# Turned probabilities in a paged decode attention: one group of 4 or 5 transposes, or one now and the rest a step later

## The chip, the cores and the metric

The kernel runs on one core of one Trainium2 chip. The metric is the device time of one launch in microseconds; the median of the runs is compared. A core has five engines that run their own instruction queues and meet by semaphores: TensorE (PE, its weight loads are shown apart as PEld), VectorE (DVE), ScalarE (ACT), GpSimd (POOL) and SyncE (SP). SP and POOL issue the transfers (DMA) here.

## What is computed

One inference step of a decoder layer for a prompt of 1024 tokens and for 8 sampled sequences of 4 new tokens each, with 8192 past positions in pages of 128. The part that the change touches is the attention of the 32 sampled tokens over their pages, in two branches: A, a softmax over the 256 keys that an indexer selected (here a bias masks the others), and B, a differential attention with two softmaxes per head.

```python
def sample_mixers(...):
    o_a = dsa_attend(qa, qi, wi, qpos, kidx_all, gather_a, topk)      # branch A
    past_b = pool_b_kv[page_table].reshape((B, P) + pool_b_kv.shape[2:])
    ...
    o_b = diff_attend(qb, segments, lam, subln_g, lam_init)           # branch B
    return o_a, o_b
def diff_attend(qb, segments, lam, subln_g, lam_init):
    ...
    p = jax.nn.softmax(jnp.concatenate(scores, axis=-1), axis=-1)
    a = p[:, :, 0] - lam * p[:, :, 1]
    ... outs.append(jnp.einsum('bhqs,bshe->bqhe', a[..., start:start + L], v))
```

Everything is float32. After the attention, a dense tail (two branch projections, the output projection, a SwiGLU block and a per-layer input) runs over all 1056 tokens.

## The kernel before

Six phases run one after the other: `project`, `prompt_select`, `prompt_attend`, `sample_select`, `sample_attend`, `tail`, with a barrier between them. The change is in `sample_attend`, which in the trace lies at about 1520 to 3280 us.

`sample_attend` walks the 8 sequences (batches `b`) in 64 chunks of 8 pages, 8 chunks a batch (`PER` = 8). For a chunk the work is: load the keys of both branches (SP, `load_keys`), transpose them on DVE (`keys`, two parts, line 1723, and `keys_a`, line 1731), multiply with the queries on PE (`scores`, lines 1563 and 1573). Four chunks fill the score banks; then ACT and DVE move them out (`evacuate`). At a batch's end the maximum is found (`top`, `top_rows`, `spread`), and ACT takes the exponentials (`exps`, line 1687). The exponentials lie with the queries on the partitions, and the product with the values wants them turned: `turn` is four 128x128 transposes on PE into the one bank `stat` (line 1603; line 1599 for the new tokens), which ACT then copies to `prob_t` (`prob_out`, line 1701; line 1698 for the new tokens). A batch has 4 such turns for its first half and 5 for its second, plus `sum` on PE (line 1610), which also writes `stat`. Every user of `stat` waits on `stat_read` for the reader of the user before it: `pe.wait_ge(stat_read, use[slot])`.

The product with the values is `values(v, part)` on PE (lines 1626 and 1630), for pages 0 to 3 (part 0) and 4 to 7 (part 1) of chunk v, ten steps (`LAG`) after the chunk's keys. The values of a chunk lie in `ring_v` and `ring_va`, which hold exactly one chunk of 8 pages. POOL loads page n into its place as soon as page n-8 has been used: `pool.wait_ge(v_used, n - RING + 1)`, in order, two transfers a page (lines 1489 and 1490, 256 KB and 64 KB). PE waits before each part for its four pages.

What sets the order on every engine is a list written by hand, `order`: for each of 74 steps the slots `scores`, `keys`, `values`, `turn` and so on. Step s holds the scores of chunk s-1, the keys of chunk s and the values of chunk s-10. Into this list a planner lays the units of the dense tail for two thirds of the tokens (`rest`: lines 1223, 1195, 1201): each slot of a step adds the same part of the step's share to a budget, and a unit is laid in when the budget covers its cost. PE, ACT, DVE and SP all walk the same list. POOL's own list of page loads doesn't follow it.

Names in the rows: `tw_w`, `tw_z`, `tw_x`, `tw_h` and `sa_t` belong to the tail units ("filler" below), `sa_s` to scores, `sa_o` to values, `sa_stat` to the shared bank. A float32 matmul of the source shows as two in the trace, so a filler of 8 in the order is x16 there.

## Time and profile before

| | us |
|---|---|
| median of 3 runs | 3784.25 |
| lowest, highest | 3779.7, 3790.87 |
| the profiled execution, its own time | 3782.91 |
| its span | 3781.3 |
| PE busy in the span | 2949.5 (78%) |
| DVE busy | 1528.3 (40%) |
| POOL busy | 589.5 (16%) |
| ACT busy | 568.1 (15%) |

The span is the profiled part of the execution; 1.6 us of its own time lie around it. Busy shares are means over phases with different limits, so the stretch of `sample_attend` is read by itself. The chain that ended last covers 14% of the span: it goes back through the phase `tail`, whose PE work is 12%, to the barrier before it.

### The profile page before, as it was taken

The numbers are of one execution on the slowest core, as the hardware profiler recorded it, in microseconds if no ns is written. First come the engines' busy times: TensorE is split into PE (matmuls) and PEld (weight loads), VectorE is DVE, ScalarE is ACT, GpSimd is POOL, SyncE is SP. The second block draws the span as 40 slices with busy tenths as digits, with TensorE's granted clock in tenths as the row PEclk, the third lists the DMA queues.
The fourth block names the chain that finished last, engine by engine and source line by source line (L and its number), as shares of the span: only waits on it lengthen the run. The fifth ranks groups of instructions, "written<-read, shape, count | busy, mean of one in ns | idle before, by whom it ended". The sixth has DMA issues, their size and how long they took to land. (4 is left out here: it accounts for less than half of the span.)

```text
span 3781.3 us, 66414 instructions
## 1 busy us (share of the span) xinstructions
PE 2949.5 (78%) x25067; PEld 1904.8 (50%) x25067; DVE 1528.3 (40%) x2849; ACT 568.1 (15%) x1201; POOL 589.5 (16%) x1089
## 2 busy tenths in 40 slices
PE   8999899369956000849888888885989888779998
PEld 4444366246756000525555655553656555446665
DVE  2222399657635883553333234344433201131102
ACT  1111200046634000010101011101101100010001
POOL 0000000000011000003343342333333442000000
PEclk9999699779968555979999989997999999889999
DMA  5232322310033004758989898997899864523333
GB/s 189 93 95 69 102 68 74 97 72 1 1 118 106 0 0 108 232 185 273 292 282 284 263 318 269 307 281 241 269 307 285 266 205 148 149 86 111 111 98 96
DMA packets 631343, 619.29 MB, mean 164 GB/s; under 512 B 64785, under 2 KB 503985, under 8 KB 630930
## 3 DMA queue, kind: packets, MB, share of 16 engines
q1 hardware_dynamic: 569106, 430.81, 37.8%
q0 software_dynamic: 61952, 184.62, 14.5%
q8 instruction: 187, 3.06, 0.4%
q14 instruction: 98, 0.80, 0.1%
HBM read 568.27 MB, written 46.98 MB: 163 GB/s over the span
## 5 line engine op out<-in xcount | busy, mean ns | idle before, releaser
L1223 PE MATMUL sa_t<-tw_z,tw_w 128*128 128x352 f32 x1664 | 559.3, 493 | 24.5 <-DVE tw_z L1301 11.1
L1723 DVE STREAM_TRANSPOSE sa_key_b<-sa_ring_k 128x2048 f32<-128x2048 f32 x128 | 295.2, 2308 | 482.7 <-PE sa_s L1563 244.6
L1489 POOL DMA_DIRECT2D sa_ring_v<-cache_b_kv x512 | 275.6, 538 | 1093.4 <-PE sa_o L1630 724.9
L1223 PEld LDWEIGHTS sa_t<-tw_z,tw_w 128*128 128x128 f32 x1664 | 330.8, 204 | 223.9 <-issue 82.6
L1223 PE MATMUL sa_t<-tw_x,tw_w 128*128 128x352 f32 x960 | 307.2, 479 | 53.8 <-DMA sa_new_sel<-new_bias 35.9
L213 PE MATMUL pr_acc<-pr_w,pr_u_t 128*128 128x512 f32 (+1 forms) x864 | 327.1, 540 | 0.0
L1490 POOL DMA_DIRECT2D sa_ring_va<-cache_a_kv x512 | 275.2, 538 | 53.7 <-issue 26.8
L1223 PEld LDWEIGHTS sa_t<-tw_x,tw_w 128*128 128x128 f32 x960 | 187.0, 198 | 163.2 <-issue 62.8
L1223 PE MATMUL ta_bank<-tp_z,tp_w 128*128 128x352 f32 x832 | 248.8, 462 | 5.6 <-DVE tp_z L1301 4.3
L213 PEld LDWEIGHTS pr_acc<-pr_w,pr_u_t 128*128 128x128 f32 x864 | 152.6, 191 | 168.2 <-issue 168.2
L439 PE MATMUL sel_g<-sel_u,sel_gw 128*128 128x352 f32 x768 | 229.6, 462 | 0.0
L1626 PE MATMUL sa_o<-sa_ring_v,sa_prob_t 128*8 128x128 f32 x4096 | 150.4, 292 | 88.4 <-DMA sa_ring_va<-cache_a_kv 86.5
L1563 PE MATMUL sa_s<-sa_key_b,sa_q_pad 32*32 32x256 f32 x8192 | 185.5, 400 | 31.0 <-DVE sa_key_b L1723 24.0
L1223 PEld LDWEIGHTS ta_bank<-tp_z,tp_w 128*128 128x128 f32 x832 | 159.1, 191 | 95.7 <-issue 8.4
L979 PE MATMUL ss_sums<-ss_count,ss_halves 128*128 128x16 f32 x66 | 20.0, 384 | 223.9 <-DVE ss_count L1052 215.5
L439 PEld LDWEIGHTS sel_g<-sel_u,sel_gw 128*128 128x128 f32 x768 | 147.0, 192 | 83.6 <-issue 3.3
L1626 PEld LDWEIGHTS sa_o<-sa_ring_v,sa_prob_t 128*8 128x8 f32 x4096 | 107.0, 94 | 141.2 <-DMA sa_ring_v<-cache_b_kv 94.5
L511 DVE TENSOR_SCALAR_CACHE_REDUCE sel_hit<-sel_score,sel_edge 128x384 f32<-128x384 f32 (+2 forms) x192 | 168.9, 942 | 3.1
L1563 PEld LDWEIGHTS sa_s<-sa_key_b,sa_q_pad 32*32 32x32 f32 x8192 | 120.1, 105 | 86.9 <-issue 31.4
L1223 PE MATMUL ta_bank<-tp_x,tp_w 128*128 128x352 f32 x480 | 143.8, 462 | 21.1 <-DMA tp_w<-w_br_a 21.1
L979 PEld LDWEIGHTS ss_sums<-ss_count,ss_halves 128*128 128x128 f32 x66 | 16.5, 309 | 227.5 <-DVE ss_count L1052 219.0
L1223 PEld LDWEIGHTS ta_bank<-tp_x,tp_w 128*128 128x128 f32 x480 | 91.9, 192 | 72.5 <-issue 22.3
(322 smaller groups left out, 3308.9 us busy)
## 6 DMA issues: line engine op xcount, KB each, us to landing
sa_ring_k<-cache_b_kv SPq DMA_DIRECT2D x512, 256.0 KB, 5.9
sa_ring_v<-cache_b_kv POOLq DMA_DIRECT2D x512, 256.0 KB, 6.1
tw_w<-w_gate_up SPq DMA_DIRECT2D x88, 512.0 KB, 8.6
sa_ring_ka<-cache_a_kv SPq DMA_DIRECT2D x512, 64.0 KB, 5.7
sa_ring_va<-cache_a_kv POOLq DMA_DIRECT2D x512, 64.0 KB, 5.9
tp_w<-w_gate_up SPq DMA_DIRECT2D x44, 512.0 KB, 3.7
tw_w<-w_down SPq DMA_DIRECT2D x32, 512.0 KB, 6.2
pr_w<-w_in SPq DMA_DIRECT2D x5, 2048.0 KB, 13.5
```

Of the source, the lines that this page charges most:

```text
L213: ins = pe.matmul(acc[c][:, 0:hi - lo], u_t[:, k, :], w[:, k, lo:hi], start=(k == 0), stop=(k == KC - 1))
L439: ins = pe.matmul(g_bank[n % 4][:, 0:PIECE], gw[j % GATE_W][:, k, :], u[:, k, c * PIECE:(c + 1) * PIECE], start=(k == 0), stop=(k == KC - 1))
L511: nc.vector.tensor_scalar(hits(i), of(i, 0, w), edge[:, n:n + 1].bitcast(F32), None, ALU.is_ge, ALU.add, accum_out=count[:, n:n + 1])
L979: pe.matmul(sums[:], halves[:], count[:], start=True, stop=True).then_inc(summed, 1)
L1223: ins = pe.matmul(bank[:, 0:PIECE], self.w[:, at % self.SLOTS, k - lo, :], moving[:, k, :], start=(k == 0), stop=(k == kc - 1))
L1489: pool.dma_start(ring_v[:, n % RING, :], rows_of(cache_b, page, 1)).then_inc(v_in[n // 4 % 2], 16)
L1490: pool.dma_start(ring_va[:, n % RING, :], rows_of(cache_a, page, 1)).then_inc(va_in[n // 4 % 2], 16)
L1563: ins = pe.matmul(s_bank[32 * h:32 * h + 32, k, 0:CH * 32], q_pad[rows, d, h, 24 - 8 * j:56 - 8 * j], key_b[rows, :, 4 * h + d, :], start= ...
L1626: pe.matmul(o_bank[32 * h:32 * h + 8, 0:P], prob_t[:, g, 0, at:at + 8], ring_v[:, g, h * P:(h + 1) * P], start=False, stop=False, tile_pos ...
L1723: nc.vector.transpose(key_b[:, at:at + 4].rearrange("p g n s -> p (g n s)"), ring_k[:, at:at + 4, :].rearrange("p g e -> p (g e)")).then_i ...
```

## The change

In a step whose number leaves 1 or 5 when divided by 8, all 4 or 5 turns of a half batch stood at the end of the step, the `sum` behind the four of the first half. Now only the first turn stands there. The others move to the next step (2 or 6): one directly after the scores, one between the two key parts, the rest and the `sum` after `keys_a`. In these next steps the two `values` parts, which stood between the key slots, come last, one directly behind the other. `finish` and `combine` stay ahead of the first turn. The numbers in `use` follow the list. As the slots of a step share its filler, the filler moves too.

```diff
+            half, turns = {1: (0, 4), 5: (1, 5)}.get(s % PER, {2: (0, 4), 6: (1, 5)}.get(s % PER, (0, 0))) if s > PER and b < NB else (0, 0)
+            begins = s % PER in (1, 5)
+            probs = [("turn", b, half, i) for i in range(turns)]
+            after = [] if begins else probs[1:]
             step = [("scores", s - 1)] if 0 < s <= CHUNKS else []
             step += [("new", b), ("set_q", b + 1)] if ends else []
+            step += after[0:1]
             step += [("keys", s, 0)] if s < CHUNKS else []
+            step += after[1:2]
...
-            step += [("values", s - LAG, 0)] if s >= LAG else []
+            step += [("values", s - LAG, 0)] if s >= LAG and not after else []
             step += [("keys", s, 1)] if s < CHUNKS else []
...
             step += [("keys_a", s)] if s < CHUNKS else []
+            step += after[2:]
+            step += [("sum", b)] if after and half == 0 else []
+            step += [("values", s - LAG, part) for part in range(2)] if s >= LAG and after else []
             step += [("spread", b)] if ends else []
-            if s % PER == 1 and s > PER:
-                step += [("finish", b - 1)] if b else []
-                step += [("combine", b - 1)] if b else []
-                step += [("turn", b, 0, i) for i in range(4)] + [("sum", b)] if b < NB else []
-            if s % PER == 5 and s > PER:
-                step += [("turn", b, 1, i) for i in range(5)]
+            step += [("finish", b - 1), ("combine", b - 1)] if s % PER == 1 and s > PER and b else []
+            step += probs[0:1] if begins else []
```

The order on PE in the first half of the second batch, from `combine` on. `x16` of line 1603 are four turns in a row. Before:

```order
440 L1641 MATMUL sa_stat<-sa_fold_b,sa_o_row 128x16
441 L1642 MATMUL sa_stat<-sa_fold_a,sa_o_row 128x32
442 L1603 MATMUL sa_stat<-sa_ident,sa_raw 128x128 x16
443 L1610 MATMUL sa_stat<-sa_total,sa_same_b 128x1 x2
444 L1610 MATMUL sa_stat<-sa_total,sa_same_a 128x1 x2
445 L1223 MATMUL sa_t<-tw_z,tw_w 128x352 x8
446 L1563 MATMUL sa_s<-sa_key_b,sa_q_pad 32x256 x64
447 L1573 MATMUL sa_s<-sa_key_a,sa_q_a 32x256 x32
448 L1223 MATMUL sa_t<-tw_z,tw_w 128x352 x8
```

The same place now (the lines are 5 higher: 1603 is 1608):

```order
443 L1608 MATMUL sa_stat<-sa_ident,sa_raw 128x128 x4
444 L1223 MATMUL sa_t<-tw_z,tw_w 128x352 x8
445 L1568 MATMUL sa_s<-sa_key_b,sa_q_pad 32x256 x64
446 L1578 MATMUL sa_s<-sa_key_a,sa_q_a 32x256 x32
447 L1608 MATMUL sa_stat<-sa_ident,sa_raw 128x128 x8
448 L1223 MATMUL sa_t<-tw_z,tw_w 128x352 x8
449 L1608 MATMUL sa_stat<-sa_ident,sa_raw 128x128 x4
450 L1615 MATMUL sa_stat<-sa_total,sa_same_b 128x1 x2
451 L1615 MATMUL sa_stat<-sa_total,sa_same_a 128x1 x2
452 L1223 MATMUL sa_t<-tw_z,tw_w 128x352 x8
```

One turn stands ahead of the scores, two in a row behind them, and one more behind a filler.

What follows on PE: the values of chunk 8, then the scores, then the values of chunk 9. Before:

```order
450 L1626 MATMUL sa_o<-sa_ring_v,sa_prob_t 8x128 x16
451 L1630 MATMUL sa_o<-sa_ring_va,sa_prob_t 32x128 x4
452 L1626 MATMUL sa_o<-sa_ring_v,sa_prob_t 8x128 x16
453 L1630 MATMUL sa_o<-sa_ring_va,sa_prob_t 32x128 x4
454 L1223 MATMUL sa_t<-tw_z,tw_w 128x352 x8
455 L1563 MATMUL sa_s<-sa_key_b,sa_q_pad 32x256 x64
456 L1223 MATMUL sa_t<-tw_z,tw_w 128x352 x8
457 L1626 MATMUL sa_o<-sa_ring_v,sa_prob_t 8x128 x16
```

Now:

```order
454 L1631 MATMUL sa_o<-sa_ring_v,sa_prob_t 8x128 x16
455 L1635 MATMUL sa_o<-sa_ring_va,sa_prob_t 32x128 x4
456 L1631 MATMUL sa_o<-sa_ring_v,sa_prob_t 8x128 x16
457 L1635 MATMUL sa_o<-sa_ring_va,sa_prob_t 32x128 x4
458 L1568 MATMUL sa_s<-sa_key_b,sa_q_pad 32x256 x64
459 L1223 MATMUL sa_t<-tw_z,tw_w 128x352 x8
460 L1631 MATMUL sa_o<-sa_ring_v,sa_prob_t 8x128 x16
```

The filler between the values of chunk 8 and the scores is gone from here; it now stands in the group of turns.

The second half of the last batch on PE, where no scores are left: the turns and the values of chunks 60 and 61. Before:

```order
L1603 MATMUL sa_stat<-sa_ident,sa_raw 128x128 x16
L1599 MATMUL sa_stat<-sa_ident,sa_raw_new 32x128 x2
L1626 MATMUL sa_o<-sa_ring_v,sa_prob_t 8x128 x16
L1630 MATMUL sa_o<-sa_ring_va,sa_prob_t 32x128 x4
L1223 MATMUL sa_t<-tw_x,tw_w 128x352 x22
L1626 MATMUL sa_o<-sa_ring_v,sa_prob_t 8x128 x16
L1630 MATMUL sa_o<-sa_ring_va,sa_prob_t 32x128 x4
L1626 MATMUL sa_o<-sa_ring_v,sa_prob_t 8x128 x16
L1630 MATMUL sa_o<-sa_ring_va,sa_prob_t 32x128 x4
```

Now:

```order
L1608 MATMUL sa_stat<-sa_ident,sa_raw 128x128 x12
L1223 MATMUL sa_t<-tw_x,tw_w 128x352 x22
L1608 MATMUL sa_stat<-sa_ident,sa_raw 128x128 x4
L1604 MATMUL sa_stat<-sa_ident,sa_raw_new 32x128 x2
L1631 MATMUL sa_o<-sa_ring_v,sa_prob_t 8x128 x16
L1635 MATMUL sa_o<-sa_ring_va,sa_prob_t 32x128 x4
L1631 MATMUL sa_o<-sa_ring_v,sa_prob_t 8x128 x16
L1635 MATMUL sa_o<-sa_ring_va,sa_prob_t 32x128 x4
L1631 MATMUL sa_o<-sa_ring_v,sa_prob_t 8x128 x16
L1635 MATMUL sa_o<-sa_ring_va,sa_prob_t 32x128 x4
```

The filler of 22 went from behind the first part of chunk 60 into the turns; both parts of chunk 60 and the first of chunk 61 now stand in a row.

## Rows read from the trace of the kernel before

**Rows 1.** Windows, whole stage: busy per engine (x instructions), PE clock, DMA share, GB/s.
```profile
1700.00:3180.00 1480.00, 1261.38 (x16985) 825.43 (x16985) 496.23 (x561) 159.07 (x285) 542.10 (x1008) 0.91 0.86 272
```
**Rows 2.** Waits, 1700 to 3180: waiter <- released by: us in total, times, longest.
```profile
POOL sa_ring_v L1489 <- PE sa_o L1630: 724.9, 72, 85.0
DVE sa_key_b L1723 <- DMA sa_ring_k<-cache_b_kv: 205.3, 28, 21.1
...
PE sa_o L1626 <- DMA sa_ring_va<-cache_a_kv: 86.5, 21, 9.7
...
PE sa_stat L1603 <- ACT sa_prob_t L1701: 30.5, 44, 0.7
```
**Rows 3.** Line 1599 on PE: idle before it, us and times.
```profile
L1599 PE MATMUL sa_stat<-sa_ident,sa_raw_new x16: 272/278/421, 1804.4 to 3112.1; 128*32 128x128 f32 x16
its engine sat idle before it (us, times) until:
  ACT sa_prob_t L1701: 4.1, 6
```
**Rows 4.** Line 1610 on PE: idle before it, us and times.
```profile
L1610 PE MATMUL sa_stat<-sa_total,sa_same_a x32: 250/250/352, 1714.2 to 3046.7; 128*128 128x1 f32 x32
its engine sat idle before it (us, times) until:
  ACT sa_prob_t L1701: 3.4, 5
```
**Rows 5.** PE timeline, turns of the second batch: start, us, what, [idle before <-releaser].
```profile
1892.88 0.66 PE L1603 MATMUL sa_stat<-sa_ident,sa_raw 128*128 128x128 f32 x4 [0.36 <-DVE sa_out_a L1799]
1894.27 0.66 PE L1603 MATMUL sa_stat<-sa_ident,sa_raw 128*128 128x128 f32 x4 [0.73 <-ACT sa_prob_t L1701]
...
1900.68 7.67 PE L1223 MATMUL sa_t<-tw_z,tw_w 128*128 128x352 f32 x16
```
**Rows 6.** PE timeline, values of chunk 8 to values of chunk 9.
```profile
1919.00 0.40 PE L1630 MATMUL sa_o<-sa_ring_va,sa_prob_t 128*32 128x128 f32 x8
1919.22 1.06 PE L1626 MATMUL sa_o<-sa_ring_v,sa_prob_t 128*8 128x128 f32 x32
1920.09 0.40 PE L1630 MATMUL sa_o<-sa_ring_va,sa_prob_t 128*32 128x128 f32 x8
1920.42 5.00 PE L1223 MATMUL sa_t<-tw_z,tw_w 128*128 128x352 f32 x16
1925.35 2.76 PE L1563 MATMUL sa_s<-sa_key_b,sa_q_pad 32*32 32x256 f32 x128
1928.04 5.00 PE L1223 MATMUL sa_t<-tw_z,tw_w 128*128 128x352 f32 x16
1933.14 1.06 PE L1626 MATMUL sa_o<-sa_ring_v,sa_prob_t 128*8 128x128 f32 x32
```
**Rows 7.** POOL timeline, the page loads that follow the values of chunk 8.
```profile
1920.36 0.54 POOL L1489 DMA_DIRECT2D sa_ring_v<-cache_b_kv  x1 [21.77 <-PE sa_o L1630]
...
1925.49 0.54 POOL L1490 DMA_DIRECT2D sa_ring_va<-cache_a_kv  x1
...
1931.55 0.54 POOL L1490 DMA_DIRECT2D sa_ring_va<-cache_a_kv  x1
```
**Rows 8.** Page, DMA issues: KB each, median us from issue to landing.
```profile
sa_ring_v<-cache_b_kv POOLq DMA_DIRECT2D x512, 256.0 KB, 6.1
```
**Rows 9.** DMA issues, 3046 to 3060, last batch: KB each, us to landing.
```profile
sa_ring_v<-cache_b_kv POOLq DMA_DIRECT2D x7, 256.0 KB, 3.5
```
**Rows 10.** PE timeline, fifth step of the second batch.
```profile
1965.14 0.40 PE L1630 MATMUL sa_o<-sa_ring_va,sa_prob_t 128*32 128x128 f32 x8
...
1978.46 1.90 PE L1626 MATMUL sa_o<-sa_ring_v,sa_prob_t 128*8 128x128 f32 x32 [4.09 <-DMA sa_ring_va<-cache_a_kv]
...
1980.71 6.92 PE L1223 MATMUL sa_t<-tw_z,tw_w 128*128 128x352 f32 x16
```
**Rows 11.** PE timeline, three more values parts 1 of such fifth steps.
```profile
2563.86 1.90 PE L1626 MATMUL sa_o<-sa_ring_v,sa_prob_t 128*8 128x128 f32 x32 [4.86 <-DMA sa_ring_va<-cache_a_kv]
...
2758.07 1.90 PE L1626 MATMUL sa_o<-sa_ring_v,sa_prob_t 128*8 128x128 f32 x32 [4.35 <-DMA sa_ring_va<-cache_a_kv]
...
2940.35 1.90 PE L1626 MATMUL sa_o<-sa_ring_v,sa_prob_t 128*8 128x128 f32 x32 [3.32 <-DMA sa_ring_va<-cache_a_kv]
```
**Rows 12.** PE timeline, fourth batch, third step, around the norm (line 1195).
```profile
2314.04 0.83 PE L1195 MATMUL sa_t<-tw_sumsq,sa_ones 128*128 128x352 f32 x2 [3.19 <-DVE tw_sumsq L1270]
...
2322.33 1.89 PE L1626 MATMUL sa_o<-sa_ring_v,sa_prob_t 128*8 128x128 f32 x32 [6.25 <-DMA sa_ring_va<-cache_a_kv]
```
**Rows 13.** PE timeline, last batch: values whose ring was only just released.
```profile
3064.86 0.40 PE L1630 MATMUL sa_o<-sa_ring_va,sa_prob_t 128*32 128x128 f32 x8
3073.97 1.89 PE L1626 MATMUL sa_o<-sa_ring_v,sa_prob_t 128*8 128x128 f32 x32 [8.71 <-DMA sa_ring_va<-cache_a_kv]
...
3112.94 1.90 PE L1626 MATMUL sa_o<-sa_ring_v,sa_prob_t 128*8 128x128 f32 x32 [0.45 <-ACT sa_prob_new L1698]
```
**Rows 14.** Windows, 24 us from the first turn of two groups.
```profile
1893.00:1917.00 24.00, 21.24 (x246) 14.05 (x247) 5.96 (x6) 2.71 (x5) 4.23 (x8) 0.79 0.55 177
...
2280.00:2304.00 24.00, 20.82 (x293) 13.99 (x294) 6.76 (x8) 3.06 (x6) 4.30 (x8) 1.00 0.60 189
```

More of the change, by code:

```diff
@@ L1430, in sample_attend @@
             ends = 0 < s <= CHUNKS and s % PER == 0
+            half, turns = {1: (0, 4), 5: (1, 5)}.get(s % PER, {2: (0, 4), 6: (1, 5)}.get(s % PER, (0, 0))) if s > PER and b < NB else (0, 0)
+            begins = s % PER in (1, 5)
+            probs = [("turn", b, half, i) for i in range(turns)]
+            after = [] if begins else probs[1:]
             step = [("scores", s - 1)] if 0 < s <= CHUNKS else []
             step += [("new", b), ("set_q", b + 1)] if ends else []
+            step += after[0:1]
             step += [("keys", s, 0)] if s < CHUNKS else []
+            step += after[1:2]
             step += [("evacuate", s // 4 - 1)] if 0 < s <= CHUNKS and s % 4 == 0 else []
             step += [("top", b)] if ends else []
-            step += [("values", s - LAG, 0)] if s >= LAG else []
+            step += [("values", s - LAG, 0)] if s >= LAG and not after else []
             step += [("keys", s, 1)] if s < CHUNKS else []
             step += [("top_rows", b)] if ends else []
-            step += [("values", s - LAG, 1)] if s >= LAG else []
+            step += [("values", s - LAG, 1)] if s >= LAG and not after else []
             step += [("keys_a", s)] if s < CHUNKS else []
+            step += after[2:]
+            step += [("sum", b)] if after and half == 0 else []
+            step += [("values", s - LAG, part) for part in range(2)] if s >= LAG and after else []
             step += [("spread", b)] if ends else []
-            if s % PER == 1 and s > PER:
-                step += [("finish", b - 1)] if b else []
-                step += [("combine", b - 1)] if b else []
-                step += [("turn", b, 0, i) for i in range(4)] + [("sum", b)] if b < NB else []
-            if s % PER == 5 and s > PER:
-                step += [("turn", b, 1, i) for i in range(5)]
+            step += [("finish", b - 1), ("combine", b - 1)] if s % PER == 1 and s > PER and b else []
+            step += probs[0:1] if begins else []
             steps.append(step)
```

## The prediction

> **What bounds the kernel now.** I read first whether TensorE paces the stage, then what it waits for. Between 1700 and 3180 us PE is busy 1261 of 1480 us while the 16 DMA engines are busy 0.86 of the time [rows 1]: PE is the pace, and the transfers are close behind. The PE queue is in order and ends the phase at a barrier, so a microsecond that PE idles less in this stage is a microsecond less in the time, unless another wait grows. The waits [rows 2] show two kinds of idle time that the change can reach. PE waits for ACT to empty the one bank `stat` between two turns: 30.5 us in 44 times before a turn, 4.1 in 6 before the turn of the new tokens [rows 3], 3.4 in 5 before `sum` [rows 4]; together 38.0 us in 55 times, 0.69 each. And PE waits for value pages: 86.5 us in 21 times [rows 2]. DVE's 205 us of waiting for keys is not on PE's path: DVE runs a chunk ahead, and none of the new steps brings the scores closer together than some 18 us.
>
> A wait for pages is set by the distance from the release of a half ring to its next use. After the values of chunk 8, part 0, end at 1919.40 [rows 6], POOL starts its first load at 1920.36 and the eighth transfer (fourth page) at 1925.49, the sixteenth at 1931.55 [rows 7]. A transfer lands 6.1 us later in the median [rows 8]; I use 6.0. So part 0 is back 0.96 + 5.13 + 6.0 = 12.1 us after its use, and part 1, when both parts are used in a row, 0.96 + 11.19 + 6.0 = 18.2 us after the use of part 0. A stall agrees: from 1965.54, where a part was released with POOL free, to 1978.46, where it was used after 4.09 us of idleness, are 12.9 us [rows 10].
>
> **What the change does, part by part.**
>
> *Handoffs.* In the order on PE, a user of `stat` that waits directly behind a turn stands 55 times before (the same 55 as in the trace) and 30 times after: other work now lies in 25 of these gaps. 25 x 0.69 = -17.3 us. `combine` directly ahead of a turn costs 0.36 [rows 5]; this stands 4 times before and 6 after: +0.7. The last turn of a second half now stands directly ahead of values at 4 more places, where PE waits for the copy, 0.45 each [rows 13]: +1.8. Sum -14.8 us. The copies on ACT and `sum`'s reader on DVE (queued behind it is the next key transposition, which waits for the scores anyway) lie beside PE work.
>
> *Value pages, the regular place.* The slots of a step share its filler, so a filler of 5.0 us that stood between the values of the second (or sixth) step and the scores now lies between the turns. What PE does from the end of part 0 to the next part 0 is now part 1, scores, filler: 1.28 + 2.76 + 5.00 = 9.0 us [rows 6]; before it was 13.7, from 1919.40 to 1933.14. Against 12.1 this is a new wait of 3.1 us (3.9 by the 12.9 of rows 10). The order shows this pattern at 9 of the 16 half batches: +28 us. Part 1 then comes 9.0 + 3.1 + 1.28 + 5.0 = 18.4 us after the use of part 0, just behind its 18.2: no second wait. If part 0 lands sooner than I say and part 1 not, the wait moves to part 1 and the sum for the place stays near 3.
>
> *The irregular places.* In the third batch a filler of 22 stays in the gap: nothing. In the fourth batch's first half the next step has only the norm in the gap, 1.28 + 2.76 + 0.83 + 3.19 = 8.1 us [rows 6, 12]: 4.0 for part 0; part 1 is reached at 8.1 + 4.0 + 1.28 = 13.4, and waits 4.8. Of these 8.9 us, 6.25 are paid now [rows 12]: +2.6. In its second half the gap is 11.4 (filler, the small units), 0.7 and then 4.8: +5.5. In the last batch the filler of 22 leaves the place behind part 0 of chunk 60 and three value parts stand in a row, as they do at 3073.97, where PE waited 8.71 [rows 13]: +8.7. The fifth batch's second half and the last batch's first half keep their gaps.
>
> *What goes.* In fifth steps the two value parts often stood in a row, and part 1 waited: 4.09, 4.86, 4.35 and 3.32 us [rows 10, 11]. At these four places a filler now lies between them: -16.6 us.
>
> *The clock.* After the turns at 1892 to 1900 the 16 matmuls of a filler took 7.67 us instead of 5.00 [rows 5, 6], with a granted clock of 0.79 over 24 us, so the lower of the two levels (1.2 GHz) for part of it; after the turns at 2280 the same stretch was granted 1.00 [rows 14]. After the stall of 4.09 us the filler took 6.92 and the values 1.90 instead of 1.06 [rows 10]. So a group of turns costs 0 to 2.7 us more than its waits, and a stall of 3 us or more some 2 to 2.8. The change thins out 16 groups and brings about nine more stalls than it takes away. 16 x 1.3 = 21 us given back against 9 x 2.3 = 21 us lost: I take zero, and keep plus and minus 15 for the range, as a group may keep half its loss and a 3 us stall may have none.
>
> Sum: -14.8 + 28 + 2.6 + 5.5 + 8.7 - 16.6 = +13.4 us. Against the profiled execution's own 3782.9 this is 3796.3; its median lies 1.3 us higher, so 3797. POOL issues the same loads in the same order, SP keeps its key loads ahead of the same scores, and the engines' work is the same: nothing else is added or removed.
>
> One rule of the notes speaks on this. The Trainium skill, DMA: Bandwidth & Descriptors, Rules for kernel authors, says to issue a transfer early, compute, and wait for it late; by it this order is worse in the third and seventh steps, since it shortens what lies between issue and wait, and the row with 4.09 us agrees. The same page, Anatomy of one DMA, gives for a transfer from POOL 2.0 us plus the bytes over 436 GB/s; that would be an estimated 2.6 us for 256 KB, part 0 back after 8.7 us, no wait at the nine places and a sum of about -15. The trace's 6.1 us median doesn't agree with it while other traffic runs.
>
> **The rivals.**
>
> *Faster: the pages land in time.* The mechanism is the landing time of the loads behind the values of second and sixth steps. The keys of the next chunk are issued early in that step and should have landed when the two value parts come, so the loads may meet a quiet memory. In the last batch, without keys, a page landed 3.5 us after issue [rows 9]. Then part 0 is back after 9.6 us and waits 0.6 at nine places (5.4), part 1 is back at 15.7 and doesn't wait, the fourth batch's places cost 0 and 3.0, the last batch 8.7: 17 us, paid by the 16.6 that go. What is left is -14.8 us: 3768 on the profile, 3769 on the median, and down to 3755 with the clock. It decides from a landing of part 0 under some 4 us together with one of part 1 under some 4.5. Against it: in the regular steps the next scores, and with them DVE and the next key loads, follow 1.3 us behind the values, so that the later loads of each part meet keys again, and the stage moves 272 GB/s in the mean [rows 1]. The page's 2.6 us would lead here too.
>
> *No change: the transfers pace the stage.* With DMA busy 0.86, what PE gains at the turns may be given back before the same pages, and the waits only move. For it: 86.5 us of page waits beside 205 us of waiting for keys on DVE. Against it: the waits fit fixed distances and not an overload. 3784, within 8.
>
> *Slower than forecast: the bunching.* The two parts of the second step and the two of the third are now released within about 20 us, beside the keys and weights. If a page then lands after 7 us, the nine places cost 4.1 each (+9 more), the others some 4 more, and the added stalls lower the clock without the turns giving it back (+20): 3830.
>
> *It doesn't do what it says.* With 30 handoffs left of 55, each still 0.7, it does so only in part; that is in the sum.
>
> **How the numbers follow.** Forecast 0.52, pages in time 0.20, no change 0.15, bunching 0.13. About 0.3% (11 us) can be told from no change. Of the forecast's cases, 3786 to 3813, I put 0.37 above 3795.6 and 0.15 below. Slower: 0.37 + 0.13 = 0.50. Same: 0.15 + 0.15 = 0.30. Faster: 0.20. The range goes from the middle of the faster case, 3763, to short of the bunching's end, 3824; the forecast's own range is 3786 to 3813.
>
> **What would show it.** Right: the waits of PE for ACT ahead of lines 1608, 1604 and 1615 come to about 21 us in 30 times; PE's waits for value pages rise from 86.5 to about 115 us, with new ones of some 3 us at part 0 of third and seventh steps, and those of fifth steps at part 1 gone. Wrong: page waits at or under 90 us (the faster rival), handoff idle above 30 us, or a growth of waits for `sa_key_b` ahead of the scores, which I have at nothing. The granted clock over the stage should stay at 0.91.

## The result: slower by 0.57%, and the profile of the changed kernel

The changed kernel takes 3802.14 us (median of 8 runs, 3796.7 to 3811.1), the kernel before, run beside it, 3779.78 (8 runs, 3770.72 to 3790.87). The ratio is 1.0057 with an interval of 1.004 to 1.0074, so the change makes the kernel slower, and by more than the measurement can miss. The profiled execution of the changed kernel took 3801.64 us with a span of 3800.0, against 3782.91 and 3781.3 before: +18.7 in the pair of profiles, +22.4 in the medians. Further down, two of e4's six executions (3815.3 and 6301.6 us) ran in a slower state, and its median, 3744.9 us, is that of the other four (3752.6 over all six).

The same stretch of the stage as in [rows 1], changed kernel (columns as there):

```profile
1700.00:3180.00 1480.00, 1255.20 (x16912) 821.95 (x16914) 495.58 (x559) 157.55 (x285) 537.58 (x1000) 0.92 0.86 271
```

PE's granted clock (0.92 for 0.91), the DMA share and the GB/s are where they were. What differs is what PE waits for. The waits on PE, changed kernel, 1700 to 3200 (us in total, times, longest); lines are 5 higher than before, so 1631 is the old 1626 and 1608 the old 1603:

```profile
PE sa_o L1631 <- DMA sa_ring_va<-cache_a_kv: 106.9, 35, 9.8
...
PE sa_s L1578 <- issue: 24.8, 13, 3.2
...
PE sa_stat L1608 <- ACT sa_prob_t L1706: 11.9, 18, 0.7
...
PE sa_s L1568 <- issue: 11.7, 7, 4.1
```

and the two rows of before that [rows 2] left out, from the same kind of view (1640 to 3180):

```profile
PE sa_s L1573 <- issue: 14.5, 9, 2.8
...
PE sa_s L1563 <- issue: 6.9, 3, 2.7
```

Against [rows 2] the page waits grew from 86.5 us in 21 times to 106.9 in 35. The handoffs at the three lines of [rows 2 to 4] fell from 38.0 us in 55 times to 20.7 in 31 (11.9 in 18, 5.4 in 8 and 3.4 in 5). And idle time that no engine and no data transfer ended, which the profile calls issue, grew from 30.7 us in 17 times to 46.7 in 26 over the whole stage (1640 to 3320), mostly ahead of score matmuls. The span grew by 18.7: PE's busy time +1.4 (2949.5 to 2950.9) and its idle time +17.3. Of that, the pages are +20.4, issue +16, the handoffs -17.3, the two small handoffs that were expected to grow +2.5 (before turns 1.5 to 2.2, before values 0.5 to 2.3), waits of the filler and of the output turns for DVE and weights about -9, and small things the rest (+5).

The regular place, changed kernel, PE timeline; it answers to [rows 6]:

```profile
1926.37 0.40 PE L1635 MATMUL sa_o<-sa_ring_va,sa_prob_t 128*32 128x128 f32 x8
1926.59 1.06 PE L1631 MATMUL sa_o<-sa_ring_v,sa_prob_t 128*8 128x128 f32 x32
1927.46 0.40 PE L1635 MATMUL sa_o<-sa_ring_va,sa_prob_t 128*32 128x128 f32 x8
1927.79 2.76 PE L1568 MATMUL sa_s<-sa_key_b,sa_q_pad 32*32 32x256 f32 x128
1930.48 5.00 PE L1223 MATMUL sa_t<-tw_z,tw_w 128*128 128x352 f32 x16
1936.07 1.06 PE L1631 MATMUL sa_o<-sa_ring_v,sa_prob_t 128*8 128x128 f32 x32 [0.59 <-DMA sa_ring_va<-cache_a_kv]
1936.94 0.41 PE L1635 MATMUL sa_o<-sa_ring_va,sa_prob_t 128*32 128x128 f32 x8
1937.28 5.00 PE L1223 MATMUL sa_t<-tw_z,tw_w 128*128 128x352 f32 x16
1945.67 1.68 PE L1631 MATMUL sa_o<-sa_ring_v,sa_prob_t 128*8 128x128 f32 x28 [3.40 <-DMA sa_ring_va<-cache_a_kv]
```

POOL's loads behind it (start, us; the eighth and the sixteenth of the two half rings):

```profile
1927.73 0.54 POOL L1494 DMA_DIRECT2D sa_ring_v<-cache_b_kv  x1 [20.41 <-PE sa_o L1635]
...
1932.86 0.54 POOL L1495 DMA_DIRECT2D sa_ring_va<-cache_a_kv  x1
...
1938.93 0.54 POOL L1495 DMA_DIRECT2D sa_ring_va<-cache_a_kv  x1
```

The filler of 5 us is gone from between part 1 and the scores. Part 0 is used again 9.3 us after its release (1926.77 to 1936.07), 0.59 us of it idle: its last load, issued at 1932.86, landed 3.07 us later. Part 1's last load is issued only at 1938.93 and landed 6.61 us later, and its values start at 1945.67 after 3.40 us of idleness. The wait of some 3 to 4 us is there, but at part 1. The trace also shows what lies between the two landings: the loads that SP issues for the next weights and keys begin at 1935.51, behind the last load of part 0 and among those of part 1.

### The profile page after: what moved, and what is told of

The parts are those of the page before. It is cut to its first block and busy times, and to the rows that moved or that the text cites. A ratio compares the mean times of both kernels' runs of the same rounds, so it can differ in the third digit from the quotient of the medians.

```text
span 3800.0 us, 66414 instructions
## 1 busy us (share of the span) xinstructions
PE 2950.9 (78%) x25067; PEld 1906.0 (50%) x25067; DVE 1528.4 (40%) x2849; ACT 566.7 (15%) x1201; POOL 589.3 (16%) x1089
## 3 DMA queue, kind: packets, MB, share of 16 engines
q0 software_dynamic: 61952, 184.62, 14.5%
## 5 line engine op out<-in xcount | busy, mean ns | idle before, releaser
L1631 PE MATMUL sa_o<-sa_ring_v,sa_prob_t 128*8 128x128 f32 x4096 | 156.6, 300 | 109.5 <-DMA sa_ring_va<-cache_a_kv 106.9
L1223 PE MATMUL ta_bank<-tp_x,tp_w 128*128 128x352 f32 x480 | 144.5, 464 | 20.7 <-DMA tp_w<-w_br_a 20.7
```

The source lines that it names most:

```text
L1223: ins = pe.matmul(bank[:, 0:PIECE], self.w[:, at % self.SLOTS, k - lo, :], moving[:, k, :], start=(k == 0), stop=(k == kc - 1))
L1631: pe.matmul(o_bank[32 * h:32 * h + 8, 0:P], prob_t[:, g, 0, at:at + 8], ring_v[:, g, h * P:(h + 1) * P], start=False, stop=False, tile_pos ...
```

## The experiments

Twelve more kernels. "The changed kernel" is that of the diff ahead, "the order before" its opposite. "Its before" is the kernel before, run beside that experiment; the span and all that stands behind it come from one profiled execution. All numbers on waits are PE's, 1640 to 3320; times at the lower of the two clock levels are read from the clock records between 1700 and 3180. Handoffs are the waits for ACT's copy at the three lines of [rows 2 to 4].

| kernel | median us | its before | ratio (interval) | span | pages us / times | handoffs | issue | lower clock us | PE busy |
|---|---|---|---|---|---|---|---|---|---|
| before | 3779.8 | | 1 | 3781.3 | 86.5 / 21 | 38.0 / 55 | 30.7 / 17 | 256 | 2949.5 |
| changed | 3802.1 | 3779.8 | 1.0057 (1.004-1.0074) | 3800.0 | 106.9 / 35 | 20.7 / 31 | 46.7 / 26 | 249 | 2950.9 |
| e1 | 3866.0 | 3783.5 | 1.0211 (1.0186-1.0236) | 3868.6 | 122.0 / 30 | 38.0 / 55 | 42.9 / 24 | 314 | 2967.3 |
| e2 | 3769.5 | 3783.5 | 0.9958 (0.9943-0.9974) | 3763.7 | 84.5 / 24 | 21.8 / 33 | 46.4 / 27 | 225 | 2931.8 |
| e3 | 3781.9 | 3783.5 | 0.9993 (0.9974-1.0013) | 3780.6 | 60.3 / 15 | 33.2 / 49 | 43.8 / 21 | 273 | 2956.7 |
| e4 | 3744.9 | 3783.5 | 0.9897 (0.9863-0.9931) | 3739.0 | 85.0 / 24 | 8.3 / 12 | 42.1 / 20 | 232 | 2933.4 |
| e5 | 3730.0 | 3778.2 | 0.9872 (0.9839-0.9905) | 3726.2 | 65.4 / 19 | 37.9 / 55 | 34.8 / 19 | 208 | 2935.9 |
| e6 | 3742.0 | 3778.2 | 0.989 (0.9866-0.9913) | 3730.5 | 90.0 / 23 | 20.7 / 31 | 41.6 / 28 | 205 | 2916.6 |
| e7 | 3673.4 | 3778.2 | 0.9702 (0.9675-0.9728) | 3676.9 | 11.8 / 2 | 38.0 / 55 | 34.9 / 17 | 197 | 2932.7 |
| e8 | 3662.5 | 3778.2 | 0.9685 (0.9659-0.9711) | 3648.2 | 10.3 / 3 | 20.7 / 31 | 58.7 / 28 | 140 | 2896.1 |
| e9 | 3786.2 | 3780.7 | 1.0023 (1.0007-1.004) | 3784.7 | 98.8 / 28 | 20.3 / 30 | 16.6 / 11 | 219 | 2966.9 |
| e10 | 3760.6 | 3780.7 | 0.9948 (0.9927-0.9969) | 3754.2 | 88.0 / 24 | 2.4 / 4 | 51.6 / 25 | 229 | 2925.6 |
| e11 | 3749.6 | 3780.7 | 0.9928 (0.9905-0.995) | 3748.4 | 81.2 / 21 | 2.1 / 3 | 17.5 / 15 | 204 | 2950.1 |
| e12 | 3736.9 | 3780.7 | 0.9894 (0.9875-0.9912) | 3742.2 | 77.5 / 20 | 8.3 / 12 | 16.8 / 14 | 201 | 2951.8 |

### Where the filler stands: e1, e2, e3

My theory was that the page waits grew because the changed order takes the filler out of the way between one use of a half ring and the next, called the distance below. The rival was that the turns, spread over two steps, or the transfers as a whole make the difference.

**e1** leaves the order before as it is, and only takes the filler from the values' places in second and sixth steps: the whole filler of these steps stands directly behind the scores.

```
+            early = step[0][0] == "scores" and (step[0][1] + 1) % PER in (2, 6) and step[0][1] >= PER
+            weight = [float(slot[0] == "scores") if early else 1.0 for slot in step]
-                budget += share / len(step)
+                budget += share * weight[n] / sum(weight)
```

> The kernel before, with one thing changed: in the steps in which the values follow a half batch's turns, the whole step's filler stands directly behind the scores, so that none lies behind the values. The turns stay in one group (55 direct handoffs). Distance theory: the values of the next step come 9.0 instead of 13.7 us after the use of part 0, so PE's waits for value pages rise from 86.5 to 105 to 120 us in some 35 times, handoff waits stay at 38 us, and the time is 25 to 35 us above the kernel before, more than the change itself, since the fifth steps keep their waits. Rival (spreading the turns, or scores between them, is what costs): the time is that of the kernel before, within 8 us.

Measured: 3865.99 us, ratio 1.0211. The waits of PE in this kernel:

```profile
PE sa_o L1628 <- DMA sa_ring_va<-cache_a_kv: 122.0, 30, 10.1
PE sa_t L1195 <- DVE tw_sumsq L1270: 73.5, 4, 24.3
PE sa_stat L1605 <- ACT sa_prob_t L1703: 30.5, 44, 0.7
```

The page waits rose by 35.5 us with the turns untouched (to 122.0 in 30 times, where 105 to 120 in 35 were expected), and the regular place shows the same distance as in the changed kernel:

```profile
1934.34 2.76 PE L1565 MATMUL sa_s<-sa_key_b,sa_q_pad 32*32 32x256 f32 x128
1937.02 5.00 PE L1223 MATMUL sa_t<-tw_z,tw_w 128*128 128x352 f32 x16
1945.09 1.06 PE L1628 MATMUL sa_o<-sa_ring_v,sa_prob_t 128*8 128x128 f32 x32 [3.06 <-DMA sa_ring_va<-cache_a_kv]
```

Here the wait falls on part 0, with the same distance. In this trace SP's loads for weights and keys begin at 1931.70, ahead of POOL's first page load at 1934.27, and the last load of part 0 took 5.55 us to land for 3.07 in the changed kernel. So where within the place the wait falls goes with when the key loads come (the section on why the prediction held counts this at all nine places); that a wait comes with this distance holds in both. The time, +82 us, is far more than the 25 to 35 I had expected: besides the pages +35.5, PE waited 21.1 us more for the norm's sums (73.5 for 52.4), 12.2 more in issue, some 5 more for keys on DVE, and was busy 17.8 us longer, with 314 us at the lower clock instead of 256. The direction and the mechanism hold; the size of the whole shows that a filler moved is never a move of one wait only.

**e2** is the changed kernel with one filler put back between the two value parts, and less of it in the turns. **e3** puts all of the turned steps' filler behind the second value part.

```
+            turned = step[1:2] and step[1][0] == "turn"
+            weight = [{"turn": 0.15, "scores": 0.15, "sum": 0.0, "values": 0.25}.get(slot[0], 0.1)
+                      if turned else 1.0 for n, slot in enumerate(step)]          # e2
+            weight = [float(slot[0] == "values" and slot[2] == 1) if turned else 1.0 ...]  # e3
-                budget += share / len(step)
+                budget += share * weight[n] / sum(weight)
```

> The changed kernel with other shares of filler in the second and sixth steps: one filler is laid between the two value parts instead of ahead of them (32 direct handoffs against 30 of the changed kernel). Distance theory: the next values come 14 us after both parts, PE's waits for value pages fall from 107 to some 75 to 85 us, handoff waits stay at 22 us, and the time is 10 to 25 us below the kernel before. Rival (spreading the turns itself costs): it stays near the changed kernel, 3795 to 3805.

> The changed kernel with all filler of the second and sixth steps laid behind the two value parts, ahead of the next scores (49 direct handoffs, some 34 us). Distance theory: the gap is 14 us and more, page waits fall to some 75 to 85 us, and with only 4 us of handoffs gained the time is 3765 to 3782, at or a little below the kernel before. Rival (two value parts in a row behind the turns are what costs): near the changed kernel, 3795 to 3805.

Measured: e2 3769.45 us (0.9958), e3 3781.94 (0.9993). Page waits of e2:

```profile
PE sa_o L1633 <- DMA sa_ring_va<-cache_a_kv: 84.5, 24, 9.5
```

and of e3, the same view:

```profile
PE sa_o L1633 <- DMA sa_ring_va<-cache_a_kv: 60.3, 15, 9.5
```

With the turns still spread over two steps, e2 brings the page waits back to 84.5 us, below those of before, and has 33 handoffs: about 1% faster than the changed kernel (ratios to before 0.9958 and 1.0057) and faster than before. So the spreading of the turns is a gain, and the distance is what it was paid with. e2 also lays less filler into the turns, so its gain belongs to the two edits together. e3 has the fewest page waits of all kernels that load whole pages, 60.3 us, but 49 handoffs, and ends level with before: pages -26.2, handoffs -4.8, but issue +13.1, busy +7.2, waits of the filler for DVE tiles (`tw_x`, `tw_h`) +11.1 and values waiting for the copy +3.1.

### What a handoff is worth: e4

Instead of moving turns, e4 takes the order before, moves one nearby filler into each group of turns where it can and cuts it into pieces, of which one stands between each two turns. 12 handoffs are left of 55.

```
+                if k < kc - 1:
+                    yield                      # Tail.tensor: a pause after each matmul
...
+                    if begun and order[order.index(slot) + 1] != ("rest", begun[0]):
+                        for _ in range(each):  # each = matmuls of the filler / turns of the group
+                            next(begun[1], None)
```

> The kernel before with its order kept, but one nearby filler of each group of turns is cut into pieces of 2 to 5 matmuls that PE issues between the turns (12 direct handoffs left of 55). Theory that the handoffs are on the path at their full size: handoff waits fall from 38 to some 8 us, page waits stay at 80 to 90, the time falls by 25 to 35 us plus what the clock gives back. Rival (the transfers pace the stage, so that PE's gain is given back in page waits): the time falls by less than 10 us and the page waits grow by as much as the handoffs lose.

Measured: 3744.9 us, ratio 0.9897. Its timeline at the group that [rows 5] shows of before:

```profile
1881.98 0.66 PE L1638 MATMUL sa_stat<-sa_ident,sa_raw 128*128 128x128 f32 x4 [0.36 <-DVE sa_out_a L1847]
1882.47 1.35 PE L1223 MATMUL sa_t<-tw_z,tw_w 128*128 128x352 f32 x4
1883.66 0.60 PE L1638 MATMUL sa_stat<-sa_ident,sa_raw 128*128 128x128 f32 x4
1884.10 1.35 PE L1223 MATMUL sa_t<-tw_z,tw_w 128*128 128x352 f32 x4
```

The four filler matmuls of the trace (two of the source, 1.35 us) cover the copy on ACT, and the 0.7 us between turns are gone. Handoffs fell by 29.7 us, PE's busy time by 16.1 (232 us at the lower clock for 256), the page waits stayed (85.0 in 24), issue rose by 11.4; the span fell by 42.3. So the page waits did not take back what the handoffs gave: a handoff on this path is worth its 0.69 us, less what issue takes. That thinning the groups out gives clock back as well is what the busy time and the clock records of this one pair say.

### Whether faster transfers would turn the verdict: e5 to e8

The rival "pages in time" said that the changed order wins if a page lands soon enough. e5 (order before) and e6 (changed) load half of each branch B page, 128 KB for 256, and leave out the values of two of the four heads: these multiply with the values of the other two. e7 and e8 also have value rings of 12 pages in three thirds. Longer rings with whole pages were not tried.

```
-        ring_v = ph.sb("ring_v", [P, RING, H_B * P])
+        ring_v = ph.sb("ring_v", [P, RING, 2 * P])                    # e5, e6
+        ring_v = ph.sb("ring_v", [P, 4 * HALVES, 2 * P])              # e7, e8: HALVES = 3
...
-                pool.dma_start(ring_v[:, n % RING, :], rows_of(cache_b, page, 1)).then_inc(...)
+                pool.dma_start(ring_v[:, n % RING, :], rows_of(cache_b, page, 1)[:, 0:2 * P]).then_inc(...)
...
-                        pe.matmul(..., ring_v[:, g, h * P:(h + 1) * P],
+                        pe.matmul(..., ring_v[:, g, h % 2 * P:(h % 2 + 1) * P],
```

> The kernel before, with the branch B values of each page loaded for two of the four heads only (128 KB instead of 256 KB a page; the other two heads use the same values, which is the part left out). As many transfers are issued by POOL, each lands sooner. Reference for the next run. Distance theory: the refill of a part still takes 0.96 + 5.1 us of POOL's issuing plus a landing of perhaps 4 us, so page waits fall from 86.5 to 40 to 60 us and the time by some 30 us.

> The changed kernel with the same halved value transfers. If the landing time decides: part 0 is back 10 us after its use, the wait at the regular places shrinks to 0 to 1 us, and the changed order is now faster than the same order before by 5 to 17 us. If POOL's issuing or something other than the pages makes the changed order slower: it stays 15 to 22 us above the halved kernel before.

Measured: e5 3729.95 us, e6 3741.96, both beside the same runs of before. The changed order is 12.0 us above in the medians and 4.3 in the spans, but the intervals of the two ratios overlap (0.9839 to 0.9905 and 0.9866 to 0.9913) and so do the single times, so which of the two is faster stays open. It is neither the 5 to 17 us of gain nor the 15 to 22 of loss that had been expected, and e5's page waits (65.4 us) lie above the expected 40 to 60. What the traces do show is what the waits did. Landing times in e6, 1700 to 3100 (KB each, median us):

```profile
sa_ring_v<-cache_b_kv POOLq DMA_DIRECT2D x495, 128.0 KB, 4.9
```

and the regular place in e6:

```profile
1918.35 1.06 PE L1631 MATMUL sa_o<-sa_ring_v,sa_prob_t 128*8 128x128 f32 x32
1919.22 0.40 PE L1635 MATMUL sa_o<-sa_ring_va,sa_prob_t 128*32 128x128 f32 x8
1919.56 5.00 PE L1223 MATMUL sa_t<-tw_z,tw_w 128*128 128x352 f32 x16
1927.71 1.90 PE L1631 MATMUL sa_o<-sa_ring_v,sa_prob_t 128*8 128x128 f32 x32 [3.15 <-DMA sa_ring_va<-cache_a_kv]
```

Part 0 waits for nothing, part 1 waits 3.15 us where it was 3.40. Half the bytes took 1.1 us off the median landing in e6 and 0.9 in e5 (5.2 for 6.1), but from the first to the sixteenth load POOL needs 11.2 us here too (1910.67 to 1921.86), and the last one landed 5.71 us after its issue, again among SP's loads of weights and keys (from 1918.45 on); with the two together part 1 is late. Page waits: 65.4 in e5, 90.0 in e6, +24.6 us, even more than the +20.4 with whole pages. The Trainium skill, DMA: Bandwidth & Descriptors, Anatomy of one DMA, gives 2.0 us plus the bytes over 436 GB/s, an estimated 2.3 us for 128 KB; the measured median is 4.9, and the five loads issued from 1910.67 to 1916.73, ahead of the key loads, took 2.65 to 3.43.

> The kernel before with halved value transfers and with rings of 12 pages instead of 8 for both branches' values, so that a part is reloaded half a chunk earlier. Distance theory: PE's waits for value pages nearly vanish (under 10 us). Reference for the next run.

> The changed kernel with halved value transfers and rings of 12 pages. With no page waits left only the handoffs differ: distance theory 12 to 20 us below the same rings with the order before, more if the thinned groups keep the clock up. Rival (the extra idle time for which the profile shows no releaser, 47 against 32 us, belongs to the changed order itself): no gain, within 5 us.

Measured: e7 3673.44 us, e8 3662.46. With a third of a ring more the page waits are all but gone in both (11.8 and 10.3 us), and the changed order is ahead, by 11.0 us in the medians (12 to 20 had been expected) and by 28.7 in the spans. The intervals of the ratios overlap, and of the five times of each only e8's slowest lies above e7's two fastest, so this is likely but not beyond the noise. The spans say more than there is: e7's profile is its slowest execution and e8's its fastest. In this pair the handoffs are -17.3, busy -36.6 (140 us at the lower clock for 197), issue +23.8. In all five executions of e8 the granted clock is higher (0.886 to 0.891) than in all of e7 (0.881 to 0.884), so the change does bring clock time where no page stall follows it, but how much of the 36.6 us is the change's own is not shown. That the page waits set the sign of this change is shown best by e2, whose gain over before is clear of the noise; e7 and e8 agree with it. What was left to explain is this row of e8, from its waits on PE:

```profile
PE sa_s L1579 <- issue: 30.5, 12, 3.7
```

In e7 the same line of the source idles 14.9 us in 7 times.

### The idle time without a releaser: e9, e11, e12

Issue idle stood in long runs of small matmuls. e9 is the changed kernel with the next filler begun inside the scores: one of its matmuls (x2 in the trace) behind each quarter of branch B's score matmuls.

```
+                    if filler and d < 3:
+                        next(filler[1])
                 ins.then_inc(scored, 1)
+                if filler:
+                    next(filler[1])
```

> The changed kernel with the same slots in the same order, but where the next filler can be begun early, one of its matmuls is issued after each quarter of a chunk's branch B scores (4 of its 8 or 22). Values, turns and their distances stay as they are. It tells what the idle time of PE without a releaser is (46.7 us in the changed kernel, 30.7 before), which stands nearly only in runs of 180 and more small matmuls without a filler. Theory that long runs of small matmuls outrun the supply of instructions: this idle time falls from 47 to 15 to 30 us and the time by 15 to 30 us; page waits stay at 100 to 110. Rival (it comes from the transfers that meet there): it stays above 40 us and the time within 6 us of the changed kernel.

Measured: 3786.23 us, ratio 1.0023. Scores in e9:

```profile
1907.01 0.71 PE L1577 MATMUL sa_s<-sa_key_b,sa_q_pad 32*32 32x256 f32 x32
1907.66 0.86 PE L1223 MATMUL sa_t<-tw_z,tw_w 128*128 128x352 f32 x2
1908.45 0.71 PE L1577 MATMUL sa_s<-sa_key_b,sa_q_pad 32*32 32x256 f32 x32
1909.09 0.86 PE L1223 MATMUL sa_t<-tw_z,tw_w 128*128 128x352 f32 x2
```

Issue fell from 46.7 to 16.6 us, and the kernel is 15.3 us shorter in span than the changed one: half of what issue gave. The other half came back elsewhere. PE's busy time rose by 16.0: in the one place compared, both at the full clock, a chunk of 128 scores with 8 filler matmuls among them takes 5.74 us here (1907.01 to 1912.75); one after the other they take 2.69 (1927.79 to 1930.48 in the changed kernel) plus half of the 4.93 us of sixteen filler matmuls (1920.42 to 1925.35 in [rows 6]), 5.16 in all. And PE waits 8.4 us more for DVE's maximum (5.1 to 13.5 in 3 times), probably since the filler that stood behind the last scores is used up inside them. The page waits gave 8.1 us. The rival of this experiment, that the idle time comes from the transfers that meet there, would have left it above 40 us.

That the idle time has to do with how the instructions are supplied can be read from the traces themselves, counted once the runs were in. Take all instructions of PE's queue in program order (weight loads, matmuls and the few others). In the changed kernel the 24 issue idles over 0.5 us (46.3 of the 46.7 us) all stand at a multiple of 256 instructions from each other, and so do the 15 of before (30.1 us). In all fourteen kernels it is 253 of 265 such idles. Beside them the trace has instruction transfers on a queue of their own (changed kernel, 1700 to 3180: packets, MB, share):

```profile
q8 instruction: 133, 2.18, 0.6%
```

These are 16.4 KB each. Counted from the same trace, for seven ends of blocks of 256:

```
block begins  PE has issued its 256 in  instruction transfer  PE idles  next block begins
1762.89       3.12 us                   1766.77 to 1767.95    3.09      1769.47
1855.22       3.39                      1859.17 to 1860.37    3.14      1861.82
1878.32       2.88                      1881.88 to 1883.01    2.73      1884.30
1953.66       2.99                      1957.39 to 1958.52    2.88      1959.90
2312.91       2.90                      2318.05 to 2319.02    4.06      2320.24
1928.10       8.20                      1928.94 to 1930.44    -         1936.30
2741.73       7.55                      2743.90 to 2744.86    -         2749.28
```

Every idle ends 1.1 to 1.7 us after such a transfer has landed (all fourteen kernels), and the new block then starts 3.7 to 7.6 us after the one before it began (four times it was 12). A block that takes PE longer than that hides its successor's transfer, as in the table's last two rows; a block of nothing but small matmuls is through in 3 us, less than the shortest of these times. Blocks passed in under 3.5 us in the stage: 23 before, 31 in the changed kernel, 32 in e6, 31 in e8, 29 in e10, 22 in e3, but 5 in e9 and e11 and 7 in e12. Over half of them idle (13 of 23, 21 of 31). The change makes more of them since a run of scores is now followed by a turn where a filler stood: runs of 180 small matmuls and more without a filler between them number 42 instead of 32 (1700 to 3010). The number of short blocks is not the whole of it: e3 and e4 have 22 and 23, as before, and yet 43.8 and 42.1 us of issue. Why a block's transfer starts 1 us after one block began and 4 or 5 us after another (the table), and so whether a short block idles for 1 us or for 4, was not settled.

The Trainium skill, Advanced Engine Details and Errata, ISA Cache, speaks of lines of 16 KB, 256 instructions, and of only two of them. The distances of 256 and the 16.4 KB agree with the first two; nothing here counts the lines. A late one costs 0.6 to 4.1 us in the changed kernel.

### The repairs put together: e10, e11, e12

e10 is e2 with e4's split fillers, e11 is e10 with e9's broken scores, e12 is e4 with e9's broken scores.

```
 e10: the weights of e2, the split of e4          e11: e10, and scores(slot[1], fresh) of e9
 e12: the order before, the split of e4, and scores(slot[1], fresh) of e9
```

> Two repairs together: the changed kernel with a filler between the two value parts (as in the second experiment, 3769 us), and one filler of each group cut into pieces between the turns (as in the fourth, 3753 us). 3 direct handoffs. If the parts add: handoff waits under 4 us, page waits 80 to 90, 3745 to 3755, no better than the fourth. If spreading the turns gives something of its own beside the handoffs (clock), 3735 to 3745.

> The tenth kernel with the scores cut by filler matmuls as in the ninth. If the three terms (handoffs, distance, idle without a releaser) are independent: 15 to 30 us below the tenth, some 3725. If not, within 6 us of the tenth.

> The fourth kernel (the order before, fillers cut into the turns) with the scores cut as in the ninth. If the idle time without a releaser is set by runs of small matmuls in the order before as well: it falls from 42 to 15 to 30 us, and the time to 3725 to 3740. Against the eleventh it tells whether any of the changed order is worth keeping: equal within 8 us if handoffs, distances and runs are all there is.

Measured: 3760.64, 3749.61 and 3736.91 us. e10 missed its 3745 to 3755: it has only 4 handoffs, but 25 issue idles with 51.6 us, 29 short blocks against 23 in e4, so that what was won at the turns (5.9 us against e4) was lost in issue (+9.5) and in waits for `tw_x` and keys (+8.8 and +9.2). e11 is 11.0 us faster than e10, where 15 to 30 had been expected: issue -34.1, but busy +24.5 and 9.2 more for DVE's maximum. e12 came to the 3725 to 3740 that had been expected, but is only as fast as e4 by the ratio (0.9894 and 0.9897): issue -25.3, pages -7.5, against busy +18.4 and DVE's maximum +10.2. And e11 is 12.7 us slower than e12, where no more than 8 had been expected if handoffs, distances and runs were all there is. So they are not all: of the two kernels e11 has 6.2 us less of handoffs, but 8.5 more of waits for `tw_x`, 5.3 for keys and 3.8 for pages. Pages and issue from e12's waits on PE:

```profile
PE sa_o L1672 <- DMA sa_ring_va<-cache_a_kv: 77.5, 20, 9.4
...
PE sa_s L1619 <- issue: 7.5, 9, 2.5
```

e4 and e12, both with the order before, beat both kernels, by 1.03 and 1.06% against before. The moving of the turns is in neither, and in neither pair that differs in it (e10 and e4, e11 and e12) did it bring anything beside the cut fillers.

## Why the prediction held, and where its terms were off

Forecast 3797.0 us, range 3763 to 3824, slower the likeliest of the three; measured 3802.1 and slower. In differences the forecast was +13.4; the profiles show +18.7 and the medians +22.4. Point by point:

- **Handoffs.** Forecast 25 fewer, -17.3, and +2.5 for `combine` and the last turn ahead of values. Measured 38.0 to 20.7 us (24 fewer), and +0.7 and +1.8. Right; e4 shows that the page waits don't take them back.
- **The regular place.** Forecast 3.1 us at nine places, +28. Measured, both parts taken together at the nine places, 31.9 us, 3.5 each, 0.6 to 5.8 per place. The size was right. Where it falls was not: I put the wait at part 0 and gave part 1 none, with a remark that it could be the other way round. At six of the nine it is (3.79, 3.71, 3.40, 3.04, 2.15 and 0.64 us at part 1, and 0 to 0.6 at part 0); at two both parts wait, and at one alone it is part 0 (5.84). The step that failed is the single landing time of 6.0 us from the median of [rows 8]. Counted from the trace of the changed kernel at the nine places: the last load of part 0 landed after 3.1 to 3.4 us at five of them, where 0 to 3 of SP's key loads were under way during it, and after 4.4 to 5.7 us at the three where part 0 waits longest (2.2 to 5.8 us), with 5 to 8 of them; that of part 1 took 6.3 to 7.2 us at these eight, with 9 to 16. The ninth place (5.0 and 5.2 us, with 1 and 0) doesn't fit. Half of the condition of "pages in time", a landing of part 0 under some 4 us, came true at five places; the other half, part 1 under some 4.5, at none. That the place still cost about 3 us is what the prediction's remark had said, but the nine differ so much that the mean of 3.5 is in part luck.
- **The irregular places.** Fourth batch, first half: forecast 8.9 us, +2.6; measured 3.81, -2.4. There PE idled for 4.06 us in the middle of the scores (the rows below), which lengthened the gap. Second half: 4.8 for 5.5. Last batch: 7.95 for 8.7.

```profile
2314.11 2.08 PE L1568 MATMUL sa_s<-sa_key_b,sa_q_pad 32*32 32x256 f32 x91
2320.24 1.55 PE L1568 MATMUL sa_s<-sa_key_b,sa_q_pad 32*32 32x256 f32 x37 [4.06 <-issue]
2324.98 1.51 PE L1195 MATMUL sa_t<-tw_sumsq,sa_ones 128*128 128x352 f32 x2 [3.18 <-DVE tw_sumsq L1270]
...
2332.22 1.90 PE L1631 MATMUL sa_o<-sa_ring_v,sa_prob_t 128*8 128x128 f32 x32 [3.81 <-DMA sa_ring_va<-cache_a_kv]
```

- **What goes.** The four waits of fifth steps, 16.6 us, are gone, as forecast. The places I had not costed lost another 5.2 us. So the pages came to +20.4 where the sum has +28.2: nine places +3.9, the fourth batch -5.8, the last -0.7, the others -5.2.
- **The clock.** Forecast zero. 256 us at the lower level before, 249 now, PE busy +1.4. Right in sum. Both sides of that zero can be seen: turns give back in e4 (-24 us at the lower level) and in e8 (-57 against e7, with the reserve named there), and the changed kernel, with 22.4 us more of page waits than e2, has 24 us more. Their sizes were not separated.
- **Missing from the sum: issue.** +16 us. It stood in the trace, 14.5 and 6.9 us in twelve times at the score lines, and I took it for constant, since no row names what ends it. With +20.4 for +28.2 at the pages, about -9 in the filler's and the output turns' waits and about +6 in small things and busy time, which I had at zero, it is what carries +13.4 to +18.7.
- **The rivals.** "Pages in time" did not come, as the page waits of 106.9 us show, and at half the bytes part 0 of the regular place waits no more, but part 1 does. The waits are nearly gone only with another third of ring (e7, e8). "The transfers pace the stage" is refuted by e2 and e4, which gain 0.4 and 1% with all transfers unchanged. "Bunching" did not come: landing is 6.0 us in the median for 6.1, and the scores wait 24.4 us for `sa_key_b` where it was 23.5.

The numbers of the forecast were right within its own range, 3786 to 3813, but partly because two misses, 8 too much at the pages and 16 too little at issue, lie on opposite sides: that part is luck, and so is that the waits of the filler took back another 9.

## What to carry over

Before moving filler from one gap to another, write down for each ring what lies between the release of a buffer and its next use, and count the issuing engine's time for a whole part, not only the landing: here the sixteen loads took 11.2 us to issue and the last one 6.6 to land, and halving the bytes left 3.15 us of wait for 3.40. And take the landing at the place itself, since other loads that come between can double it. A short wait for a copy is better filled where it stands, by cutting a filler into pieces, than by moving the waiting work as it was moved here (e4 against the change: 1.0% faster instead of 0.6% slower). And idle time that the profile ascribes to issue is not a constant: count it before and after, and look at how long the runs of small instructions become.

## What the hardware did that I had not expected

- PE's instructions arrive in blocks of 256. When PE passes a block in under 3.5 us, in over half of the cases it idles at its end until the next has come, 0.6 to 4.1 us; all of the larger issue idles of both kernels stand at such ends (24 and 15 of them). Neither half the bytes per value page (34.8 us of issue in e5, 41.6 in e6) nor longer rings (34.9 and 58.7 in e7 and e8) took it away.
- Breaking such runs with large matmuls gives half of the gain back on PE: 16.0 us of busy time in e9, and 0.58 us in the chunk of scores that was compared (5.74 for 5.16).
- Two loads that POOL issues 6 us apart on the same queue differed in landing by a factor of two (3.07 and 6.61 us), the later one among SP's key loads, so that a median over the stage says little about one place.
- The time at the lower clock is 314 us in e1 with the most page waits and 140 in e8 with the fewest and only 31 handoffs; PE's busy time is 71 us apart between these two for the same number of matmuls. The idle gaps alone don't give it: e3 has fewer page waits and handoffs than before and 273 us for 256. Why was not found.
